# Gated linear attention with one chunk for each 128-token tile instead of two of 64

## The reference, cut to what matters

```python
# N = T // 64 chunks; qf, kf, vf, g: (B, H, N, 64, d)
b = jnp.cumsum(g, axis=3)                  # within the chunk
b_last = b[..., -1:, :]
q_t, k_t, k_h = qf * exp(b), kf * exp(-b), kf * exp(b_last - b)
A = where(tri, einsum('bhnid,bhnjd->bhnij', q_t, k_t), 0)
o_intra = einsum('bhnij,bhnjv->bhniv', A, vf)
kv_chunk = einsum('bhnjd,bhnjv->bhndv', k_h, vf)
# over the chunks: S_prev of a chunk is S, then S = exp(b_last) * S + kv_chunk
o = o_intra + einsum('bhnid,bhndv->bhniv', q_t, S_prev)
```

## Time and profile before

| | |
|---|---|
| runs | 1357.07 us, median of 3 (1356.28 to 1357.45) |
| span of the profiled execution | 1357.1 us |
| TensorE busy | 1272.0 us, 94% |
| VectorE busy | 846.9 us, 62% |
| ScalarE busy | 564.7 us, 42% |
| GpSimd busy | 172.4 us, 13% |
| mean granted clock of TensorE | 0.968 |

### The profile page before, as it was taken

One profiled execution on the slowest core, in us unless ns is written; L12 is line 12 of the kernel. 1 busy time (PEld: TensorE's weight loads), 2 busy tenths in 40 slices (PEclk: granted clock), 3 DMA queues, 4 the chain that ended last, 5 costly groups with the idle time before them and its releaser, 6 DMA issues. The chain is left out here.

```text
span 1357.1 us, 24773 instructions
## 1 busy us (share of the span) xinstructions
PE 1272.0 (94%) x9778; PEld 1188.9 (88%) x9778; DVE 846.9 (62%) x1356; ACT 564.7 (42%) x933; POOL 172.4 (13%) x216
## 2 busy tenths in 40 slices
PE   7999998999988997899999799999998999999896
PEld 7987787888767776799999799999998999999896
DVE  4212222345597776576797777777757666668978
ACT  3212323133645445635654445445464333333425
POOL 3424333010000000023100000000000000000653
PEclk9999998999889998999999899999999999999998
DMA  7748888333312002153226676766698655554103
GB/s 287 229 138 287 280 272 283 109 94 94 104 39 51 10 1 94 32 168 99 79 87 237 218 282 235 267 238 235 244 311 307 212 187 188 184 181 145 53 9 118
DMA packets 110713, 226.92 MB, mean 167 GB/s; under 512 B 12756, under 2 KB 60134, under 8 KB 106503
## 3 DMA queue, kind: packets, MB, share of 16 engines
q1 hardware_dynamic: 104454, 208.56, 44.8%
q0 software_dynamic: 6144, 16.79, 4.0%
HBM read 165.54 MB, written 58.73 MB: 165 GB/s over the span
## 5 line engine op out<-in xcount | busy, mean ns | idle before, releaser
L2750 PE MATMUL psum<-step_hid_hi,step_w_hi 128*128 128x258 f32 x784 | 159.2, 284 | 7.9 <-DVE y_sums L2799 3.8
L355 PE MATMUL psum<-xTh,win_hi 128*128 128x344 f32 (+1 forms) x432 | 149.7, 347 | 9.6 <-DVE xTl L408 9.6
L2750 PE MATMUL psum<-step_hid_hi,step_w_lo 128*128 128x258 f32 x784 | 158.5, 284 | 0.0
L2750 PE MATMUL psum<-step_hid_lo,step_w_hi 128*128 128x258 f32 x784 | 157.8, 283 | 0.0
L355 PE MATMUL psum<-xTl,win_hi 128*128 128x344 f32 (+1 forms) x432 | 141.3, 327 | 0.0
L355 PE MATMUL psum<-xTh,win_lo 128*128 128x344 f32 (+1 forms) x432 | 141.1, 327 | 0.0
L2750 PEld LDWEIGHTS psum<-step_hid_hi,step_w_hi 128*128 128x128 f32 x784 | 122.7, 191 | 8.8 <-DVE step_w_lo L2725 4.1
L2750 PEld LDWEIGHTS psum<-step_hid_hi,step_w_lo 128*128 128x128 f32 x784 | 122.0, 190 | 0.0
L2750 PEld LDWEIGHTS psum<-step_hid_lo,step_w_hi 128*128 128x128 f32 x784 | 121.5, 190 | 0.0
L2401 PE MATMUL psum<-x_t_hi,w_variant_hi 128*128 128x258 f32 x512 | 104.9, 287 | 11.8 <-DVE product_sums L2495 10.9
L355 PEld LDWEIGHTS psum<-xTh,win_hi 128*128 128x128 f32 (+1 forms) x432 | 83.2, 193 | 24.8 <-issue 24.3
(11 more groups left out here) (406 smaller groups left out, 3026.7 us busy)
## 6 DMA issues: line engine op xcount, KB each, us to landing
hid_rows<-hid_variants SPq DMA_DIRECT2D x14, 1806.0 KB, 6.9
step_hid_raw<-hid_rows SPq DMA_DIRECT2D x21, 1032.0 KB, 7.6
k_pages<-in_pages SPq DMA_DIRECT2D x128, 160.0 KB, 3.1
v_pages<-in_pages POOLq DMA_DIRECT2D x128, 128.0 KB, 4.3
w_raw<-in_w SPq DMA_DIRECT2D x16, 1024.0 KB, 5.2
step_w_raw<-w_sums SPq DMA_DIRECT2D x12, 1024.0 KB, 5.1
step_w_raw<-in_w SPq DMA_DIRECT2D x9, 1024.0 KB, 5.3
win_raw<-in_w_in SPq DMA_DIRECT2D x17, 512.0 KB, 6.9
```

Of the source, the lines that this page charges most:

```text
L355: mm = pe.matmul(psum[0:M, 3 * (m % 2) + b, 0:BLK], w[:, m % 2, k, 0:M], x[:, k, b * BLK:(b + 1) * BLK], start=(k == 0 and i == 0), stop=( ...
L2750: mm = pe.matmul(slot(d)[:, s, :], wt[r][:, w], ht[r][:, TH * f + s * BW:TH * f + (s + 1) * BW], start=(f == 0 and i == 0), stop=(f == G - ...
```

## The change

A chunk is now the whole 128-token tile. The sums `b` are taken relative to the tile's middle, by a constant matrix whose entries are +1/16 from token 64 up to the output's token and -1/16 for tokens below 64 that come after it; a further column gives the sum of the first half. `exp_b` gets that column too (130 columns instead of 128). The same `k_tilde` now serves both the scores and the key-value products, so `k_hat_T` with its copy, difference, exponential and product is gone. The state is kept relative to the next tile's middle: VectorE adds the product to the state and scales it by two decay columns. `kv` is one result in place of two. Its four matmuls have full 128x128 weights: `k_rows` holds for each head the 64 key columns beside 64 columns of zeros, which GpSimd clears once. The state part of the output is one full matmul per head in place of two of 64 tokens.

```diff
-            names = (("cum",), ("A",), ("kva", "kvb"), ("v",), ("kh",), ("O",))[r]
+            names = (("cum",), ("A",), ("kv",), ("v",), ("kh",), ("O",))[r]
...
-        khT = sb(at, "k_hat_T", [P, 2, 2, P]); at += 4 * P
-        kh = sb(at, "k_hat", [P, 2, 2 * P]); at += 4 * P
+        kh = sb(at, "k_rows", [P, 2, 2, 4, DK]); at += 8 * P
...
-                    mm = pe.matmul(o[:, f * P:(f + 1) * P], loga[:, t, f * P:(f + 1) * P], const("tri16"), start=True, stop=True)
+                    mm = pe.matmul(o[:, f * 130:(f + 1) * 130], loga[:, t, f * P:(f + 1) * P], const("tri16")[:, 0:130], start=True, stop=True)
...
-                pe.wait_ge(khm_done, t + 1)
+                pe.wait_ge(kt_done, t + 1)
                 for f in range(2):
-                    mm = pe.transpose(o[:, f * P:(f + 1) * P], khT[:, i, f, :], ident)
+                    mm = pe.transpose(o[:, f * P:(f + 1) * P], kt[:, i, f, :], ident)
...
-                        mm = pe.matmul(o[half(hh), f * DV:(f + 1) * DV], kh[r, i, h * DK:(h + 1) * DK],
-                                       gv[r, i, h * DV:(h + 1) * DV], start=True, stop=True)
+                        mm = pe.matmul(o[:, f * DV:(f + 1) * DV], kh[:, i, f, 2 * hh:2 * hh + 2, :].rearrange("p n c -> p (n c)"),
+                                       gv[:, i, h * DV:(h + 1) * DV], start=(hh == 0), stop=(hh == 1))
             elif name == "O":
-                gb.read(pe, ("A", t)), gb.read(pe, ("kvb", t))
+                gb.read(pe, ("A", t)), gb.read(pe, ("v", t))
+                if t:
+                    pe.wait_ge(gstate_done, t)
                 for h in range(HEADS):
-                    f = h // 2
-                    pe.matmul(o[:, h * P:(h + 1) * P], am[:, i, h, :], gv[:, i, h * P:(h + 1) * P], start=True, stop=True,
-                              skip_group_check=True)
-                    for c in range(2):
-                        mm = pe.matmul(o[CH * c:CH * c + CH, h * P:(h + 1) * P], qt[:, i, f, h % 2, CH * c:CH * c + CH],
-                                       hist[:, (2 * t + c) % 4, f, :], start=False, stop=True, skip_group_check=True)
+                    pe.matmul(o[:, h * P:(h + 1) * P], am[:, i, h, :], gv[:, i, h * P:(h + 1) * P], start=True, stop=False)
+                    mm = pe.matmul(o[:, h * P:(h + 1) * P], qt[:, i, h // 2, h % 2, :], hist[:, i, h // 2, :], start=False, stop=True)
...
-            if r == 1 and t < 8:
-                act.wait_ge(sub_done, t + 1)
-                act.activation(khT[:, t % 2], khT[:, t % 2], ACT.Exp).then_inc(seen_done, 1)
...
+                gb.free(dve.tensor_tensor(supd[:], gb.of(key)[:, 0:2 * DV].rearrange("p (f v) -> p f v", f=2), hist[:, i], ALU.add), key)
...
+                        ins = dve.tensor_scalar(hist[:, t % 2, f, :], supd[:, f, :], c_last, eb[:, t % 2, f, P:P + 1], ALU.mult, ALU.mult)
...
             pool.memset(qt[:], 0.0).then_inc(gz_done, 1)
+            pool.memset(kh[:], 0.0).then_inc(gz_done, 1)
...
+    put("tri16", np.where(t < P, (i <= t) - before_mid, np.where(t == P, before_mid, 0.0)) / 16.0)
+    put("tilemask", i <= j)
```

More of the change, by code:

```diff
@@ L63 @@
 _at = 0
-for _n, _w in (("ident", P), ("ones", P), ("swap", P), ("tri16", P), ("chunkmask", P), ("causal", P),
-               ("dup", P), ("swapdup", P), ("pad", 272), ("sel4", 4), ("rowmask", 1), ("half", 2), ("end", 1)):
+for _n, _w in (("ident", P), ("ones", P), ("swap", P), ("tri16", 136), ("tilemask", P), ("causal", P),
+               ("dup", P), ("swapdup", P), ("pad", 264), ("sel4", 4), ("rowmask", 1), ("half", 2), ("end", 1)):
     CONST_COLS[_n] = (_at, _w)
@@ L791, in hymba_step @@
         zabs_done, ln_done, lg_done = sem("gate_abs"), sem("gate_ln"), sem("loga_done")
-        exb_done, sub_done, seen_done, khm_done, qt_done = (sem("gla_" + n) for n in ("exps", "b_differences", "exp_hat", "k_hat", "q_tilde"))
+        exb_done, kt_done, qt_done, gstate_done = (sem("gla_" + n) for n in ("exps", "k_tilde", "q_tilde", "state"))
         ebs_done, ks_done, kz_done, st_done, os_done, osn_done = (sem("sample_" + n) for n in (
@@ L1072, in dve_slot @@
             t, r = s // 6, s % 6
[L1073 to L1084, removed]
             if r == 1:
@@ L1089, in dve_slot @@
                     if t == 1:
-                        dve.wait_ge(gz_done, 3)
+                        dve.wait_ge(gz_done, 4)
                     if t >= 3:
@@ L1098, in dve_slot @@
                     dve.wait_ge(gqk_loaded[i], 16 * (t // 2 + 1))
[L1099 to L1116 removed]
+                    gb.read(dve, ("cum", t))
                     if t == 0:
@@ L1120, in dve_slot @@
                         gb.wait(dve, ("O", t - 2))
-                    dve.tensor_tensor(kt[:, i], kt[:, i], gqk[:, i, 2:4, :], ALU.mult)
+                    dve.tensor_tensor(kt[:, i], kt[:, i], gqk[:, i, 2:4, :], ALU.mult).then_inc(kt_done, 1)
                     for hh in range(2):
                         ro = half(hh)
-                        ins = dve.scalar_tensor_tensor(qt[ro, i, :, hh, :], gqk[ro, i, 0:2, :], DK ** -0.5, eb[ro, i], ALU.mult, ALU.mult)
+                        ins = dve.scalar_tensor_tensor(qt[ro, i, :, hh, :], gqk[ro, i, 0:2, :], DK ** -0.5, eb[ro, i, :, 0:P], ALU.mult, ALU.mult)
                     ins.then_inc(qt_done, 1)
+            if r == 2 and 1 <= t <= 8:
+                key, i = ("kv", t - 1), (t - 1) % 2
+                gb.wait(dve, key)
+                if t >= 2:
+                    dve.wait_ge(gstate_done, t - 1)
+                    gb.wait(dve, ("O", t - 2))
+                gb.free(dve.tensor_tensor(supd[:], gb.of(key)[:, 0:2 * DV].rearrange("p (f v) -> p f v", f=2), hist[:, i], ALU.add), key)
+                gb.read(dve, key)
+                if t < 8:
+                    dve.wait_ge(exb_done, t + 1)
+                for f in range(2):
+                    c_last = eb[:, i, f, P - 1:P]
+                    if t < 8:
+                        ins = dve.tensor_scalar(hist[:, t % 2, f, :], supd[:, f, :], c_last, eb[:, t % 2, f, P:P + 1], ALU.mult, ALU.mult)
+                    else:
+                        ins = dve.tensor_scalar(hist[:, t % 2, f, :], supd[:, f, :], c_last, None, ALU.mult)
+                ins.then_inc(gstate_done, 1)
             if r == 3 and s % 12 == 3 and s // 12 < 3:
@@ L3104, in _tables @@
     put("swap", (i ^ (ROPE // 2)) == j)
-    same = i // CH == j // CH
-    put("tri16", (same & (i <= j)) / 16.0)
-    put("chunkmask", same & (i <= j))
+    t = np.arange(136)[None, :]
+    before_mid = (i < P // 2) * 1.0
+    put("tri16", np.where(t < P, (i <= t) - before_mid, np.where(t == P, before_mid, 0.0)) / 16.0)
+    put("tilemask", i <= j)
     put("causal", np.where(j <= i, 0.0, NEG))
```

50 lines of the change are left out of this document (18 added, 32 removed).

## The result

The changed kernel takes 1341.03 us (median of 6 runs, 1337.45 to 1342.28), the kernel before beside it 1357.01 (6 runs, 1350.42 to 1359.85). The ratio is 0.9874, 95% interval 0.9853 to 0.9895: 16 us less, where 13.7 were forecast. The span of the profiled execution went from 1357.1 to 1339.0 us.

A forecast was written before the change was run, and what follows sets the result against it. TensorE was taken as the bound up to about 347 us, then a chain over three engines. Savings 8.5 - 0.1 + 1.1 + 3.7 = 13.2 us took 1357.1 to 1343.9, a third of a low-clock stretch to 1343.4; range 1339.0 to 1348.5.

The forecast's parts named there:

- the sum: Whole stage: savings of 8.5, 1.1 and 3.7 us less a loss of 0.1, together 13.2 us.
- Output block: TensorE, tiles 0 to 5: eight full matmuls at 0.20 us save 1.42 us a block, 8.5 us in six.
- Key-value block: TensorE: four full matmuls cost 0.81 us for 0.79, a loss of 0.1 us over seven blocks.
- Banks: TensorE's PSUM bank waits: those before `uv` and `sv` go, 1.1 us together; 1.0 before two `so` stays.
- A as a whole: From the projection matmul ahead of tile 0's score block to the one ahead of tile 6's: 9.5 us saved.
- End of the stage: From 346.9 us on: VectorE's copy of output block 7 and all behind it come 3.7 us earlier.
- The third of a low stretch that I counted: Low clock at 335.30 us costs about 1.4 us; a third counted as gain, moving 1343.9 to 1343.4.
- The clock gives more: Rival, chance 0.25: the low stretch at 335 and part of the one from 359.2 go; 1340.5 us.
- Part given back: Rival, chance 0.23: end of stage yields only 0.8 of 3.7 us, later stages get another low stretch; 1347.8.
- no shrinking: Rival, chance 0.04: output block keeps its cost, 8.5 us and two thirds of the 3.7 are missing; 1354.
- Slower: Rival, chance 0.03: low clock after the projection outlasts its 20.5 us and eats the gain; up to 1361.
- signs of being right: Trace signs, including gaps, waits, first rotary matmul 13 us earlier than 380.13, and the same distance from there to the end.

The follow-up runs named there:

- before_again: The kernel before, unchanged, traced a second time; 1352.59 us, one run.
- after_again: The changed kernel, unchanged, run and traced again; 1340.93 us, ratio to the kernel before 0.9884.
- half_O: The changed kernel with the state part of each output block again two half-width matmuls per head; 1345.53 us, ratio to the kernel before 0.9926.
- before_full_O: The kernel before with one full-width state matmul per head, using only the first chunk's state; 1347.2 us, ratio 0.9923.
- kv_64: The changed kernel with key-value matmuls of 64 weight columns, each head into its half of the partitions; 1340.33 us, ratio to the kernel before 0.9874.
- two_banks: The changed kernel with the four key-value matmuls in two results, two places of the bank list; 1350.33 us, ratio to the kernel before 0.995.

## Why the prediction was right, step by step

The forecast was 1343.4 us, the range 1339.0 to 1348.5, the result 1341.03. Between before_again and after_again, which had about the same stretches at half clock in the stage, S fell by 129.69 - 116.22 = 13.5 us; the sum had said 13.2. Part of this agreement is luck: A gave 1.0 us more than the sum had for it, and the end of the stage 1.0 less.

- *Output block.* 1.42 us forecast, 1.34 measured; six give 8.0 for 8.5. The new matmul costs 0.21 and not 0.20. Shown from both sides, by half_O and before_full_O. (The 0.16 us between projection matmuls was read from one to the first of the score block; between two projection matmuls it is 0.16 as well, as from 273.01 to 273.16 in half_O.)
- *Key-value block.* Forecast 0.02 dearer, measured 0.96 for 0.95. The first one was 0.5 cheaper, which I had not priced: in the kernel before, `kvb` of tile 0 took the gap to 1.43. kv_64 shows the small form 0.12 cheaper. By the Trainium skill (TensorEngine Tiling (Array Packing), Tiling Modes) small tiles can run side by side, which by the expectation of kv_64 would be a gap of 0.6. The trace, with 0.84, doesn't show that for a block of four between full ones.
- *Banks.* `uv` and `sv`: gaps 2.75 for 3.42 and 1.41 for 1.97, together 1.2 for 1.1. The two `so` were to stay at 1.0 us of waits. They fell to 0.3; the blocks with them are 0.23 and 0.29 shorter. VectorE frees the earlier `so` sooner than I worked out. two_banks shows that the place in the list is the cause of the waits before `uv`, `sv` and `sO`.
- *A* as a whole: 84.50 - 74.00 = 10.5, for 9.5.
- *End of the stage.* Forecast 3.7, measured 31.31 - 28.58 = 2.7 between the two later traces, and 5.9 against the first. Several single steps came as said: VectorE's row went from 7.13 to 6.47 us (0.66 for 0.8; the two scalings took 0.60 of length and 0.52 from start to start, for 0.4), `v` and `kh` of tile 7 wait, and `nk` waits for ScalarE and starts 1.5 us earlier than in the first trace, for 1.7. One term was wrong in kind. Of the 3.7, 1.4 were the copy's wait for output block 7. before_again shows that at full clock there is no such wait in the kernel before, so the shorter block gave nothing there. The other 2.3 fit: counted from the start of B, the copy comes at 24.1 us in before_again and at 20.6 in the changed kernel. Of these 3.5, before_again lost 1.2 to a stretch at half clock on its last projection matmuls (the last one starts at 10.7, for 9.5 in the first trace). And from the copy to the first rotary matmul the changed kernel takes 8.0 us for 7.2, since more of its last transposes and broadcasts run at half clock. So the 2.7 is a difference of three parts, and two of them are the clock's.
- *Base and clock.* I took the span of 1357.1 for the time of the runs. The timed runs lie some 2 us above their spans (1341.03 for a span of 1339.0, 1352.59 for 1350.4), so that execution was about 2 us longer than most of its kernel. The forecast did not move by it, since the runs' median was 1357.07 as well. The execution's stage was 5.0 us longer than that of before_again. The third of a low stretch that I counted was the right sign for a wrong reason: the stretch at 335 is absent in before_again too.
- *What the stage does not explain.* The change did 2.3 us better than forecast. The mean granted clock over the 32 runs of the kernel before is 0.9705, over 12 of the changed kernel 0.9729. With 8 us for 0.01, as among the 32, that is some 2 us, an estimate. Single pairs of traces can't show it: C gave 0.3 us back in one and 4.4 in the other. Whether the closer matmuls cause the higher clock no run shows.
- *The rivals.* "The clock gives more", at 1340.5, named the measured time better than the forecast did. Both its signs came in the first pair of traces, where the stretch at 335 and most of the one from 359 are gone; but before_again lacks them without the change, so that they are gone is no work of the change. What stays of it is the 2 us above. Part given back and no shrinking are out. Slower is out: from 358 to 378 the clock is 0.98. Of the signs of being right, two did not come as written: the first rotary matmul was 22.5 us earlier than 380.13 and not 13, and from there to the end it took 4.4 us longer. Both lie in the difference between the two executions.

## What to carry to other kernels

Where one engine is full, price a change by the start-to-start gap of its neighbours around the block, and take the price of the new form from a block of the same form: both came within 0.1 us. When results go through a few banks in turn, count what stands two places back for every neighbour of a key that is added or removed. And compare stages between traces, from one fixed instruction to another; a second trace of the kernel before would have shown 5 us of chance in the stage at the price of one run, and that a wait which the forecast took out was there only at half clock. Compare the mean granted clock of all runs as well: it differed by 0.002 to 0.003 between kernels here, and that is 2 to 2.5 us of their medians.

## What was not expected of the hardware

Two half-width fp32 matmuls into separate halves of the partitions, set between full-width ones, cost far more than the one full-width matmul that does the work of both: a head takes 0.76 us with one full and two half, 0.43 with two full ((1.86 - 0.16) / 4). In half_O the full one, with the half form behind it, takes 0.42 us from start to start (274.00 to 274.42), where in a block of full ones it takes 0.22, and the pair takes 0.37. So about half of the extra cost falls on the full matmul beside the change of form, and the pair takes longer than the one full matmul does. In a row of their own they are not dearer: four matmuls of 64 columns take 0.68 us net (0.84 - 0.16), four full ones 0.80. The matmuls of half_O are also summed onto the full one's result, those of kv_64 are not; no run separates the summing into halves from the change of form.

The same kernel spent 20.5 us at half clock behind the projection in one execution. In the other it had 3.4 us there (0.92 over the stretch of 20.5 us) and 3.4 us just ahead of the projection's end; with it B was 3.2 us shorter. The kernel with the half-width blocks, 7 us slower by its median, had the higher mean clock of the two (0.976 for 0.973).
